# A mixture of experts on one core: the three full rounds and the four half-size rounds merged into one list of steps

## What is computed

```python
def moe_swiglu(h, w_router, w_gate, w_up, w_down):
    logits = (xf @ w_router).astype(jnp.float32)
    top_logits, top_idx = lax.top_k(logits, TOP_K)      # 2 of 8 experts a token
    gates = jax.nn.softmax(top_logits, axis=-1)
    ...
    def expert_block(args):
        tok, e = args
        xb = xf[tok]
        hb = jax.nn.silu(xb @ w_gate[e]) * (xb @ w_up[e])   # 1024 -> 3584
        return hb @ w_down[e]                               # 3584 -> 1024
    ...
    out = jnp.zeros((T, D), jnp.float32).at[row_tok].add(y)
```

## Time and profile before

| | before |
|---|---|
| median of 3 runs | 1929.42 us (1928.87 to 1932.44) |
| the profiled execution | 1926.18 us, span 1924.4 us |
| PE busy | 1788.7 us, 93% of the span |
| DVE busy | 1520.4 us, 79% |
| ACT busy | 1232.8 us, 64% |
| POOL busy | 265.4 us, 14% |

### The profile page before, as it was taken

One profiled execution on the slowest core, in us unless ns is written; L12 is line 12 of the kernel. 1 busy time (PEld: TensorE's weight loads), 2 busy tenths in 40 slices (PEclk: granted clock), 3 DMA queues, 4 the chain that ended last, 5 costly groups with the idle time before them and its releaser, 6 DMA issues.

```text
span 1924.4 us, 24601 instructions
## 1 busy us (share of the span) xinstructions
PE 1788.7 (93%) x8738; PEld 1482.7 (77%) x8738; DVE 1520.4 (79%) x1806; ACT 1232.8 (64%) x1446; POOL 265.4 (14%) x297
## 2 busy tenths in 40 slices
PE   8989998899989899999889999999989898998887
PEld 6867877688869788888878888888767676777766
DVE  7775996858667654454878888888999999999998
ACT  5562145755664454434766777777888888888876
POOL 4113302314011000000009600000000101010100
PEclk9999999999999999999999999999999999999999
DMA  9422334314415255554159999999999999999996
GB/s 354 159 88 88 109 138 152 132 68 173 154 66 197 88 197 197 180 191 175 62 229 355 369 377 394 374 390 375 371 421 402 406 422 412 422 412 422 411 422 280
DMA packets 74276, 511.78 MB, mean 266 GB/s; under 512 B 9392, under 2 KB 9408, under 8 KB 14272
## 3 DMA queue, kind: packets, MB, share of 16 engines
q1 hardware_dynamic: 70736, 498.88, 66.1%
q0 software_dynamic: 3440, 11.58, 2.0%
HBM read 503.08 MB, written 7.36 MB: 265 GB/s over the span
## 4 chain that ended last, share of the span: by engine, by line
PE 56%; DVE 20%; DMA 11%; ACT 7%; issue 5%; POOL 1%; DVEq 0%; SPq 0%; ACTq 0%; POOLq 0%
PE psum L1080 31%; DVE low L1034 11%; DMA raw<-in_moe_weights 10%; PE psum L1474 6%; PE psum L1488 6%; PE psum L1481 6%; ACT high L1031 4%; DVE arena L2213 3%; PE psum L2054 2%; PE psum L1514 1%; PE psum L1519 1%; ACT h L1789 1%; PE psum L3860 1%; PE psum L3863 0%; DVE small L1833 0%
## 5 line engine op out<-in xcount | busy, mean ns | idle before, releaser
L1034 DVE TENSOR_TENSOR low<-raw,high 128x2048 fp32r<-128x2048 f32 x459 | 1038.8, 2286 | 230.5 <-ACT high L1031 226.3
L1031 ACT ACTIVATE high<-raw 128x2048 fp32r<-128x2048 f32 x459 | 873.9, 1911 | 315.9 <-PE psum L1080 150.4
L1080 PE MATMUL psum<-high,yT_high 128*128 128x512 f32 x1616 | 462.6, 401 | 55.3 <-DVE yT_high L4082 50.5
L1080 PE MATMUL psum<-low,yT_high 128*128 128x512 f32 x1616 | 450.1, 398 | 7.9 <-DVE low L1034 5.3
L1080 PEld LDWEIGHTS psum<-high,yT_high 128*128 128x128 f32 x1616 | 298.1, 191 | 126.3 <-issue 45.4
L1080 PEld LDWEIGHTS psum<-low,yT_high 128*128 128x128 f32 x1616 | 302.7, 190 | 92.8 <-DVE low L1034 30.5
L1080 PE MATMUL psum<-high,yT_low 128*128 128x512 f32 x776 | 219.4, 390 | 0.0
L1080 PEld LDWEIGHTS psum<-high,yT_low 128*128 128x128 f32 x776 | 145.6, 188 | 30.9
L1474 PE MATMUL psum<-high,hT_high 128*128 128x512 f32 (+2 forms) x464 | 124.5, 389 | 0.7 <-issue 0.5
L1481 PE MATMUL psum<-low,hT_high 128*128 128x512 f32 (+2 forms) x464 | 122.5, 385 | 0.1
L1488 PE MATMUL psum<-high,hT_low 128*128 128x512 f32 (+2 forms) x464 | 122.1, 385 | 0.0
(11 more groups left out here) (443 smaller groups left out, 1873.9 us busy)
## 6 DMA issues: line engine op xcount, KB each, us to landing
raw<-in_moe_weights SPq DMA_DIRECT2D x336, 1024.0 KB, 9.3
raw<-in_weights SPq DMA_DIRECT2D x132, 1024.0 KB, 4.8
raw<-in_weights SPq DMA_DIRECT2D x2, 896.0 KB, 4.5
raw<-in_weights SPq DMA_DIRECT2D x2, 768.0 KB, 5.9
x<-in_x SPq DMA_DIRECT2D x2, 512.0 KB, 3.8
raw<-in_weights SPq DMA_DIRECT2D x2, 512.0 KB, 3.7
base<-x POOLq DMA_DIRECT2D x1, 1024.0 KB, 6.7
rows<-arena POOLq DMA_DIRECT2D x1, 1024.0 KB, 4.9
```

The source lines that it names most:

```text
L1031: eng.activation(high, raw, ACT.Copy).then_inc(k.high_ready, 1)
L1034: eng.tensor_tensor(low, raw, high.bitcast(F32), ALU.subtract).then_inc(k.low_ready, 1)
L1080: last = pe.matmul(out, lhs[:, c, :], rhs[:, c, :], start=start and c == 0, stop=stop and c == chunks - 1)
```

## The change

The rounds 0 to 2 and the rounds 3 to 6 run side by side. Every item now has its round in its name, and `moe_order()` merges two lists. The big rounds are alone for their first 16 granules (`ALONE`); from there on an item of the big list or of the small one is taken, whichever keeps the two in proportion (110 big granules beside 168 small ones), until round 7 follows alone. The small list begins with the `gather` of round 3, so the first rows that POOL fetches are now those of round 3.

```diff
+def round_order(t):
...
+        if j == FF_STEPS and t not in (BIG - 1, LAST, "more"):
+            order += [(t + 1, "gather", 0), (t + 1, "gather", 1)]
...
+def moe_order():
+
+    size = {"gate": 2, "up": 2, "down": 2, "down first": 1, "down second": 1}
+    big = [item for t in range(BIG) for item in round_order(t)]
+    small = [(BIG, "gather", 0), (BIG, "gather", 1)] + [item for t in range(BIG, N_EXPERTS) for item in round_order(t)]
+    beside_big = sum(size.get(kind, 0) for _, kind, _ in big) - ALONE
+    beside_small = sum(size.get(kind, 0) for t, kind, _ in small if t != LAST)
+    order, done_big, done_small = [], 0, 0
+    while big or small:
+        lead = done_big < ALONE or (done_big - ALONE) * beside_small <= done_small * beside_big
+        if big and (lead or not small):
+            item = big.pop(0)
+            done_big += size.get(item[1], 0)
+        else:
+            item = small.pop(0)
+            done_small += size.get(item[1], 0)
+        order.append(item)
+    return order
```

```diff
+    for t in (0, BIG):
+        for half in range(2):
+            banks.plan(("moe", t, "expert", half), Banks.LONG)
...
-    b.silu = k.carve(2, FF_STEP)
-    b.hidden = k.carve(2, FF_STEP)
-    b.rows = k.carve(D)
+    b.silu = [k.carve(2, FF_STEP) for _ in range(2)]
+    b.hidden = [k.carve(2, FF_STEP) for _ in range(2)]
+    b.rows = [k.carve(D) for _ in range(2)]
...
+    b.pair_tokens = free.high[:, 0:D].rearrange("p (c n) -> p c n", c=KC)
+    b.pair_hidden = free.low[:, 0:2 * FF_STEP].rearrange("p (t n) -> p t n", t=2)
```

PE waits for the fetched rows where the `gather` stands in the merged list, and POOL follows the same list:

```diff
+    if kind == "gather":
+        if j == 0:
+            pe.wait_ge(k.gathered[spot.pairs], 16 * (spot.turn + spot.pairs))
+        turn_rows(k, pe, b.rows[spot.pairs], name, j)
...
+    fetch(BIG)
+    for t, kind, j in MOE_ORDER:
+        if kind == "gate" and j == 0 and t != LAST:
+            take_weight(t)
+            if t != BIG - 1:
+                fetch(t + 1)
+        if kind == "out":
+            add_rows(t)
```

More of the change, by code:

```diff
@@ L407 @@
 UNSCALED = (0, 2, 3, 5)
[L410 removed]
+MOE_SHORT = 2 + sum(kind not in DOWN for _, kind, _ in MORE_ORDER)
 assert MOE_SHORT % 4 == 0
@@ L3500, in split_one, with granule_number, load_expert_part @@
-def split_one(k, eng, i, t):
+MOE_GRANULES, MOE_HALVES = granules_of(MOE_ORDER)
+MORE_GRANULES, MORE_HALVES = granules_of(MORE_ORDER)
+ROUND = len(MORE_GRANULES)
+PLACE_IN_ROUND = {granule[1:4]: i for i, granule in enumerate(MORE_GRANULES)}
+assert ROUND % RAW == 0 and ROUND % SPLIT == 0 and len(MOE_GRANULES) == ROUND * N_EXPERTS
+def granule_number(k, n, r=None):
+    first = k.granules[-1].number + 1 + n
+    return first if r is None else first + len(MOE_GRANULES) + ROUND * r
+def load_expert_part(k, sp, n, expert, part, r=None):
+    sp.wait_ge(k.low_ready, granule_number(k, n - RAW, r) + 1)
+    slot = (k.first_granule["moe"] + n) % RAW
+    one = k.w["moe_weights"][expert:expert + 1, part] if isinstance(expert, int) else k.w["moe_weights"][bass.ds(expert, 1), part]
+    sp.dma_start(k.raw[:, slot, :], one.rearrange("e p n -> (e p) n")).then_inc(k.landed[slot], 16)
@@ new lines, in moe_scalar, with whole_round @@
+    done = SPLIT
+    for index, (t, kind, j) in enumerate(MOE_ORDER):
+        if (kind, j) != ("turn", FF_STEPS - 1):
+            done = split_upto(k, act, done, MOE_GRANULES, index)
+        step(Spot(t), kind, j)
+    last_out(Spot(LAST))
+    def whole_round(r):
+        spot, done = Spot("more", r), SPLIT
+        for n in range(SPLIT):
+            split_expert_part(k, act, n, r)
+        for i in range(2):
+            gather_scalar(k, act, b, spot.name("gather", i), i, spot.more)
+        for index, (_, kind, j) in enumerate(MORE_ORDER):
+            if (kind, j) != ("turn", FF_STEPS - 1):
+                done = split_upto(k, act, done, MORE_GRANULES, index, r)
+            step(spot, kind, j)
+        last_out(spot)
@@ new lines, in last_out @@
+    def last_out(spot):
+        for half in range(2):
+            out, cols = spot.name("expert", half), slice(512 * half, 512 * (half + 1))
+            v.wait_ge(k.last_high, half + 1 if spot.r is None else 2 * spot.r + half + 3)
+            k.release(v.tensor_tensor(b.out.low[:, cols], k.bank(out), b.out.high[:, cols].bitcast(F32), ALU.subtract), out)
+    done = SPLIT
+    for index, (t, kind, j) in enumerate(MOE_ORDER):
+        if (kind, j) != ("turn", FF_STEPS - 1):
+            done = split_upto(k, v, done, MOE_GRANULES, index)
+        step(Spot(t), kind, j)
@@ new lines, in whole_round @@
+    def whole_round(r):
+        spot, done = Spot("more", r), SPLIT
+        expert = table_entry(k, v, r + 1)
+        put(expert, 1)
+        for n in range(SPLIT):
+            split_expert_part(k, v, n, r)
+        for i in range(2):
+            gather_vector(k, v, b, spot.name("gather", i), i, spot.more, spot.more_parts)
+        for index, (_, kind, j) in enumerate(MORE_ORDER):
+            if (kind, j) != ("turn", FF_STEPS - 1):
+                done = split_upto(k, v, done, MORE_GRANULES, index, r)
+            step(spot, kind, j)
+        last_out(spot)
```

592 lines of the change are left out of this document (279 added, 313 removed).

## The result

The changed kernel takes 1943.37 us (median of 5 runs, 1940.03 to 1946.67), the kernel before 1929.42 (5 runs, 1928.87 to 1932.44). The ratio is 1.0075, with a 95% interval of 1.0057 to 1.0092: slower by 14 us, where 1926.0 and a small gain had been predicted. The profiled execution took 1946.12 us, its span 1944.2.

The account below looks back on a forecast made before the run. Rounds 0 to 6 were taken as bound by PE in big rounds and the weight stream in small. Rows at 1096, restart 1106, 666 stream, 24.5 traffic, 3 to PE, 3 allowance: round 7 at 1802.5 (-3.5), median 1926 us, range 1914 to 1944.

Parts of the forecast that it names:

- what binds: Rounds 0 to 6 merged: the weight stream sets the pace at 422 GB/s, 2.485 us a granule; PE and DVE fit under it.
- the stall: PE at round 3's gather, behind granule 17, waits for POOL's row fetch, from 1067.5 to 1096 us; 44 us at POOL's old pace.
- 710.5 us: Stream time from granule 18 to round 7: 276 granules at 2.485 us, 686, plus 24.5 of row traffic; 28 less than before.
- PE at the gather at 1067.5: Time in us at which PE was to reach round 3's gather, behind granule 17, and begin waiting for its rows.
- The rows at 1096: Landing time of round 3's rows fetched by POOL, chosen between 1091 at the earliest and 1111.8 at the latest.
- both reasons: Why POOL speeds up in the stall: its instructions shorten once DVE is still, its small DMAs land sooner without weight traffic.
- The stream's restart: Behind round 3's gather: 10 us from the rows' landing until a `raw` slot is free and weights load again, at 1106.
- the allowance of 3 us for times at which DVE makes SP late: Merged stretch up to round 7: 3 us added to 1799.5 because DVE is 95% full, giving 1802.5.
- Edits of storage and semaphores cost nothing: Merged rounds: each step keeps the same instructions, so these edits add 0 us; one PE wait is the only addition.
- a `turn` gets items of the other list between itself and its `down`, so its latency hurts less: Merged list: argument, without a size, against the rival of engines that trip each other.
- the rival of engines that trip each other: Merged stretch: waits leave DVE idle over 5%, 2.60 us a granule, round 7 at 1818.6, 1942 us; chance 0.17.
- The median: Whole kernel: median 3.2 us above the profiled execution of 1922.7, so 1926 us.

Follow-up runs that it names:

- `e1_rule`: Changed kernel, but ACT and DVE may refill ahead of `turn 6` where other-list items stand between `down first` and it: 1922.88 us, 0.9980 of the kernel before.
- `e6_rule_rows_early`: `e1_rule` plus round 3's rows filled by a plain DMA before the lists are made (wrong tokens, same work): 1908.93 us, 0.9901 of the kernel before.
- `e3_together`: Changed kernel with `down first`, `turn 6` and `down second` of a round kept adjacent in the merged list, refill rule unchanged: 1924.05 us, 0.9981 of the kernel before.
- experiment 3: Changed kernel with the refill of `e1_rule` in the small rounds only, tabled place by place against `e1_rule`: 1933.74 us, 1.0041 of the kernel before.
- the rows' edit: Round 3's rows filled by a plain DMA before the lists, first indirect fetch removed (wrong tokens); alone on the changed kernel: 1932.33 us, 1.0021 of the kernel before.
- The half dose: The kernel of experiment 3: changed kernel, early refill for small rounds only, big rounds keep the late one: 1933.74 us, 1.0041 of the kernel before.
- `e10_gather_sooner34`: `e1_rule` with 34 big granules alone instead of 16 and round 3's gather one item earlier: 1906.46 us, 0.9902 of the kernel before.
- `e7_rule_alone32`: `e1_rule` with 32 big granules alone instead of 16: 1911.55 us, 0.9917 of the kernel before.

## Why the prediction was wrong

The time lies at the upper end of the range from 1914 to 1944 us, but the kernel moved the other way: 3.5 us less were forecast and 14 more measured. By the traces round 7 begins at 1824.8 and not at 1802.5, 22.3 us late, and what lies behind its start takes 1.1 us longer than before.

**Right: what binds.** The merged list does run at the stream's rate, 411 to 421 GB/s in the slices that have neither the stall nor a parted turn, except the one with 387 (400 in `e1_rule`), and PE and DVE fit under it. 710.5 us were worked out for 276 granules without a stall. `e6_rule_rows_early` takes 714.3 from its gather to round 7, with a gap of 4.4 in it. The gain of the mixture is there; two losses of some 20 us each cover it, of which the stall was counted in and the other was not.

**Right: the stall.** PE at the gather at 1067.5 was off by the drift of this execution (granule 0 5 us later, the granules up to the gather 1.6 us slower), which the stall swallowed. The rows at 1096 were right to 0.2 us, and with both reasons: POOL's instructions are short once DVE is still, and the landings are shorter. That it was so exact is in part luck, since 1096 was a choice between 1091 and 1111.8. The Trainium skill's rule in "SBUF — State Buffer" (section "SBUF: two separate sides"), that a DVE instruction with two SBUF inputs and a GpSimd instruction that reads SBUF have the shared port pair in turn, fits the trace: the issue beside the subtraction takes 2.84 us, those after it 0.95 to 1.00. In `e1_rule` and `e3_together` the last subtraction is over 1.5 us before the first issue, and that one takes 1.15 and 1.16. The stream's restart was counted at 1106; the queue of SP has it at 1106.4:

```profile
1106.41 4.75 SPq L3532 DMA_DIRECT2D raw<-in_moe_weights  x3
```

**Wrong, and the step that failed: the allowance of 3 us for times at which DVE makes SP late.** From the landing to round 7 the forecast was 706.5 us (1096 to 1802.5). `e1_rule` takes 709.2 (1095.66 to 1804.89), the changed kernel 728.6. So the terms of the sum held together but for this one. It was 3 and would have to be 25: 5.7 without the parted turns, and 19.4 for them (20.5 by the count from granule 0). And what was late was not SP behind DVE: in the changed kernel DVE is idle for 7.8% of the stretch (670.13 of 726.50 us busy), against 5.3% in `e1_rule`, where ACT may refill the slots. The waits of ACT between 1115 and 1800 us (total, times, longest):

```profile
ACT arena L3984 <- PE psum L3908: 11.7, 4, 6.6
ACT arena L3976 <- PE psum L1118: 8.9, 5, 4.3
ACT yT_high L3979 <- PE psum L3911: 5.8, 2, 5.1
```

The third row is the turn of a big round; its 5.1 us are those of round 1. In `e1_rule` the first of them is 5.8, 3, 2.5 and the others are not listed. Their sum is no measure of the cost, though: the kernel before has 12.1, 4, 4.7 for the first kind. What a place costs is in the table of experiment 3. The allowance was a guess at a queue in steady state; what was missed is a single rule, in a line that the change rewrote with the same sense as before. The prediction said "Edits of storage and semaphores cost nothing: each step has the same instructions". The instructions are the same, but their order on ACT and DVE is not a copy of the list of items: it is worked out from it by `until`, which holds a place in the list. An item put in front of that place makes the producers wait for it too.

**Wrong: "a `turn` gets items of the other list between itself and its `down`, so its latency hurts less".** For `turn 0` to `turn 5` items do come in there; whether it helps no run shows. For `turn 6` the items came in between it and `down first`, and there they hurt. This stood as an argument against the rival of engines that trip each other, which was priced at 2.60 us a granule and 1942 us, given 0.17, and came out at 2.63 and 1943. Its condition, waits for PE that leave DVE idle for over 5%, was met with 7.8%. But its reason, three engines too near their limit, was not the right one: in `e1_rule` DVE fills 95% of the stretch (669.35 of 707.10) and PE 97%, and the stream still runs at 411 GB/s on average. That the rival's time came out is luck.

**The median.** The profiled execution was to be 3.2 us under the median; here it is 2.7 us over it. The difference in front of the experts alone is up to 5.7 us between executions of the same code, more than the effect that was forecast.

**Open.** By the medians the rows' edit is worth 11 us with the parted turns and 14 without, by the traces 17.5 both times behind granule 0. Less the 2.2 to 2.4 us in front of it the traces leave some 15. The medians without parted turns agree with that to 1 us; those with them fall 4 us short of it. The half dose lies 10.9 us above `e1_rule` by the medians, 11.7 by the ratios, where its trace says 7.2. The traces are one execution each, so some 4 us of this kind stay unexplained. Not tried was a faster making of the lists, which would allow fewer granules alone: at 0.31 us each, 16 of them are worth 5 us at most.

## What to carry to other kernels

When two lists of work are merged, look at everything that is worked out from a place in the list, above all at how far ahead a producer may run: print the producer's order and compare it, not only the order of the consumer. Where two resources are each nearly full, price every standstill of either at its full length, and look for them one by one at the seams of the work (round ends, gathers), since a lump allowance doesn't find them. And before a change is given up because it came out slower, compare its good stretches with the forecast: here 11 of the 16 slices behind the stall, the last one apart, had the 411 to 421 GB/s that were hoped for, and three small edits made 14 us of loss into 19 us of gain.

## What the runs showed of the hardware

- GpSimd's indirect DMA issues are longer beside a DVE subtraction with two SBUF inputs. The four that write the places took 2.04 to 3.27 us where DVE kept working (the kernel before, `e10_gather_sooner34`) and 0.96 to 1.16 where it stood (`e1_rule`, `e3_together`). In the changed kernel the first one overlaps DVE's last subtraction and ends 1.02 us behind it.
- The small DMAs were waited for less long in the stall: the indirect writes of the places 1.42 to 3.34 us and the read back 1.58 to 1.64 (`e3_together`, `e1_rule`, the changed kernel), against 5.60 to 5.96 and 5.79 to 6.17 beside the weight stream (`e10_gather_sooner34`, the kernel before). Stream and DVE stood at the same time there, so which of them makes it is not shown.
- On a gather whose rows are there, the way from the transposes over ACT and DVE back to PE takes 3.83 to 4.39 us, as granules queue in front of the short splits. Behind such a gap matmuls ran at the lower clock: the first four of 512 columns took 2.05 us in `e7_rule_alone32` (granted clock 0.50 from 1117.7 to 1120, the lower of the two levels), and 1.17 in `e10_gather_sooner34`, without the gap (granted clock 1.00).
- One core's weight stream from memory held 421 to 422 GB/s in whole slices of 48 us, and 417 on average over 668 us with POOL's row traffic in them (`e10_gather_sooner34`, 1114.7 to 1782.7).
- Granule 0 began at 1017.3 to 1023.0 us in kernels that do the same up to there.
